# A router product turned round: weights stationary in four column groups, partial sums folded by stacked identities

## The reference

```python
x = x + gate1 * (concat(y_A, y_B) @ w_out)
h = rmsnorm(x, g_norm2) * (1.0 + scale2) + shift2
probs = softmax(h @ w_router)                 # 16 experts
gates, idx = top_k(swapaxes(probs, 1, 2), cap)  # each expert picks: 64 latent, 16 context tokens
# 16 SwiGLU experts on the picked rows, added back with their gates
```

## Time and profile before

| | |
|---|---|
| median of 3 runs | 897.25 us (895.78 to 897.99) |
| the profiled execution | 896.64 us |
| its span on the core | 894.2 us |
| TensorE busy | 97% of the span |
| granted TensorE clock, mean | 0.995 |
| output projection and routers of tiles 0 to 3 | from about 265 to 325 us |
| choice of the largest | 325.7 to 338.4 us |
| experts | from 344.8 us to the end |

### The profile page before, as it was taken

How to read it: one execution, slowest core, us unless ns; L and a number is a source line. 1 busy time by engine, 2 the same in 40 slices (tenths; PEclk the granted TensorE clock), 3 DMA queues, 4 the chain that set the end, 5 groups by cost and what they waited for, 6 DMA issues and landing times.

```text
span 894.2 us, 14324 instructions
## 1 busy us (share of the span) xinstructions
PE 869.4 (97%) x6263; PEld 484.3 (54%) x6263; DVE 288.2 (32%) x592; ACT 226.4 (25%) x437; POOL 84.5 (9%) x83
## 2 busy tenths in 40 slices
PE   5999999999999999999999999999999999999995
PEld 4798999999998885333333333333333333333332
DVE  3476553767465564201101101101101101101125
ACT  5557633462351224101101101101101101101123
POOL 1000000000000012011011011011011011011022
PEclk9999999999999999999999999999999999999998
DMA  9845714523248348999999999999999999999973
GB/s 350 298 151 185 256 65 151 200 96 119 82 145 357 132 153 321 362 386 409 399 384 411 409 386 410 399 386 412 394 381 413 395 384 412 395 381 410 422 253 132
DMA packets 48577, 272.37 MB, mean 305 GB/s; under 512 B 6283, under 2 KB 8367, under 8 KB 36229
## 3 DMA queue, kind: packets, MB, share of 16 engines
q1 hardware_dynamic: 40716, 255.15, 72.3%
q0 software_dynamic: 6128, 10.89, 5.2%
q10 hardware_dynamic: 1672, 5.43, 1.6%
HBM read 257.95 MB, written 14.55 MB: 305 GB/s over the span
## 4 chain that ended last, share of the span: by engine, by line
PE 93%; DVE 3%; ACT 1%; issue 1%; DMA 1%; ACTq 0%; POOLq 0%; POOL 0%; DVEq 0%
PE pair L2143 25%; PE pair L1799 16%; PE pair L2188 13%; PE pair L2173 13%; PE pair L2201 6%; PE pair L2014 5%; PE pair L1739 2%; PE pair L1834 2%; PE pair L2102 1%; PE pair L2158 1%; PE pair L1778 1%; PE pair L1942 1%; PE pair L2027 1%; PE pair L2164 1%; PE pair L1847 1%
## 5 line engine op out<-in xcount | busy, mean ns | idle before, releaser
L2143 PE MATMUL pair<-ring,xT 128*64 128x512 f32 x1024 | 223.9, 594 | 0.3 <-ACT xT L1017 0.3
L2143 PEld LDWEIGHTS pair<-ring,xT 128*64 128x64 f32 x1024 | 71.9, 137 | 142.1 <-issue 141.9
L2173 PE MATMUL pair<-ring,xT 128*32 128x512 f32 x1024 | 116.5, 595 | 0.9 <-DVE xT L1604 0.9
L2188 PE MATMUL pair<-ring,aT 128*64 128x512 f32 x512 | 116.9, 598 | 0.0
L1039 ACT ACTIVATE act_l<-pair 128x512 f32<-128x512 f32 x16 | 9.6, 597 | 290.8 <-PE pair L2143 290.8
L1613 DVE TENSOR_TENSOR act_l<-act_l,pair 128x512 f32<-128x512 f32 x16 | 11.0, 686 | 207.9 <-ACT act_l L1039 207.9
L1799 PE MATMUL pair<-hT_hi,w_hi 128*128 128x320 f32 x320 | 75.4, 317 | 1.5 <-DVE hT_lo L1183 1.5
L1799 PE MATMUL pair<-hT_lo,w_hi 128*128 128x320 f32 x320 | 73.1, 310 | 0.0
L1799 PE MATMUL pair<-hT_hi,w_lo 128*128 128x320 f32 x320 | 72.9, 309 | 0.0
L2188 PEld LDWEIGHTS pair<-ring,aT 128*64 128x64 f32 x512 | 34.0, 136 | 69.5 <-issue 68.2
L2173 PEld LDWEIGHTS pair<-ring,xT 128*32 128x32 f32 x1024 | 30.2, 109 | 73.1 <-issue 73.1
(11 more groups left out here) (299 smaller groups left out, 937.0 us busy)
## 6 DMA issues: line engine op xcount, KB each, us to landing
ring<-in_w_gate SPq DMA_DIRECT2D x32, 2048.0 KB, 29.2
ring<-in_w_up SPq DMA_DIRECT2D x32, 2048.0 KB, 18.1
ring<-in_w_down SPq DMA_DIRECT2D x32, 2048.0 KB, 23.7
p1w<-in_w_mod SPq DMA_DIRECT2D x12, 2048.0 KB, 10.6
p1w<-in_w_in SPq DMA_DIRECT2D x5, 2048.0 KB, 8.0
x_sb<-in_x_sample SPq DMA_DIRECT2D x8, 512.0 KB, 5.2
p1w<-in_w_out SPq DMA_DIRECT2D x2, 2048.0 KB, 8.3
hn<-xr ACTq DMA_DIRECT2D x5, 512.0 KB, 2.6
```

The lines of the kernel that those rows point to most:

```text
L2143: ins = mm(ps[64 * n:64 * n + 64, :], xt[:, kk, 0:CAP_L], w[:, j, n * 512:(n + 1) * 512], start=kk == 0, stop=kk == KC - 1)
L2173: ins = mm(ctx_ps[32 * g:32 * g + 32, :], xt[:, kk, CAP_L:96], w[:, j, n * 512:(n + 1) * 512], start=kk == 0, stop=kk == KC - 1)
L2188: ins = mm(y_ps[0][r:r + 64, :], aT[:, j, 64 * fh:64 * fh + 64], wd[:, j, n * 512:(n + 1) * 512], start=fh == 0 and j == 0, stop=fh == 1 a ...
```

## The change

The router is turned round. The scaled weights, padded with zeros from 16 to 32 columns, become stationary, and the 128 turned tokens move. Row k goes to column group k mod 4, so a tile's result comes as four partial sums in four bands of 32 PSUM rows, experts along partitions (job `lp{t}`). These 128x128 are copied to SBUF (`parts`: by ScalarE for tiles 0, 1, 2 and 4, by VectorE for tile 3), and one further product with `parts` stationary and `group_sum` moving (four stacked identities, 128x16) adds the four bands and turns the result back (job `lg{t}`, in the second bank of the same pair). `group_sum` is made by a reduction of the identity. `normalise(3)` and `store_rows(3)` move behind the first softmax. Around `router(4)` four more identity products are put in. The semaphore `silu_zero` is folded into `const_ready`. In the diff below the parts follow in the order: list of jobs, memory, ScalarE, VectorE, TensorE.

```diff
-    jobs += ["wo0", "wo1", "x2T0", "x2T1", "lg0", "wo2", "lg1", "x2T2", "wo3", "lg2", "x2T3", "lg3", "pT", "wo4", "g2_0", "g2_1", "ixT", "x2T4", "lg4", "pTc", "ixTc", "pcT"]
+    jobs += ["wo0", "wo1", "x2T0", "x2T1", "lp0", "wo2", "lg0", "lp1", "lg1", "x2T2", "wo3", "lp2", "lg2", "x2T3", "lp3", "lg3", "pT", "wo4", "g2_0", "g2_1",
+             "ixT", "x2T4", "lp4", "lg4", "pTc", "ixTc", "pcT"]
...
-        w_scaled = at("w_scaled", R_V + 4096, [P, KC, 2, E])
+        w_scaled = at("w_scaled", R_V + 4096, [P, KC, 2, 32])
+        group_sum = at("group_sum", R_V + 6144, [P, E])
+        parts = at("parts", R_V + 6656, [P, 2, P])
...
+            def router_parts(t):
+                act.wait_ge(job_done, job(f"lp{t}") + 1)
+                if t >= 2:
+                    act.wait_ge(job_done, job(f"lg{t - 2}") + 1)
+                a.activation(parts[:, t % 2, :], pairs[PAIR[f"lg{t}"]][:, 0:P], ACT.Copy).then_inc(part_ready, 1)
+
             for t in range(NT - 1):
                 second_norm(t)
                 if t + 2 < NT:
                     mixed_hi(t + 2)
+                if t:
+                    router_parts(t - 1)
                 if t == NT - 2:
                     h2_turn(t)
                     a.activation(smax[:, 0, NT - 1:NT], one_col[:, 0:1], ACT.Exp)
-                store_rows(t)
                 if t < NT - 2:
+                    store_rows(t)
                     h2_turn(t)
...
             a.activation(probs[:, 0:NT - 1, :], probs[:, 0:NT - 1, :], ACT.Exp).then_inc(exp_ready, 1)
+            store_rows(NT - 2)
...
             h2_turn(NT - 1, 1)
+            router_parts(NT - 1)
...
+            dve.wait_ge(const_ready, 2)
+            v.memset(w_scaled[:, :, :, E:], 0.0)
+            v.tensor_reduce(group_sum[:, :], ident[:, :].rearrange("p (g e) -> p e g", g=4)[:, 0:E, :], AX.X, ALU.add)
             for i in range(2):
-                ins = v.tensor_tensor(w_scaled[:, :, i, :], w_router_sb[:, :, :],
+                ins = v.tensor_tensor(w_scaled[:, :, i, 0:E], w_router_sb[:, :, :],
                                       scale2[:, :, i:i + 1].to_broadcast([P, KC, E]), ALU.mult)
...
-                v.scalar_tensor_tensor(out=logits[:, t, :], in0=pp[:, 0:E], scalar=rms[:, 5, t:t + 1],
+                v.scalar_tensor_tensor(out=logits[:, t, :], in0=pp[:, 512:512 + E], scalar=rms[:, 5, t:t + 1],
...
                 inverse_of(rms, slice(t, t + 1), EPS)
-                normalise(t)
                 if t < NT - 2:
+                    normalise(t)
                     high_chunks(t)
                 if t:
                     router_row(t - 1)
+            dve.wait_ge(job_done, job(f"lp{NT - 2}") + 1)
+            dve.wait_ge(job_done, job(f"lg{NT - 4}") + 1)
+            v.tensor_copy(parts[:, (NT - 2) % 2, :], pairs[PAIR[f"lg{NT - 2}"]][:, 0:P]).then_inc(part_ready, 1)
             router_row(NT - 2)
...
+                if turn == 1:
+                    normalise(NT - 2)
                 pp = result(dve, ("pT", "pTc")[turn - 1])
...
                 for k in range(KC):
-                    ins = mm(pp[:, 0:E], h2T[t % 2][:, k, :], w_scaled[:, k, vec(t), :], start=k == 0, stop=k == KC - 1)
-                end(ins, f"lg{t}")
+                    g = 32 * (k % 4)
+                    ins = mm(pp[g:g + 32, 0:P], w_scaled[:, k, vec(t), :], h2T[t % 2][:, k, :], start=k < 4, stop=k >= 4)
+                end(ins, f"lp{t}")
+
+            def router_sum(t):
+                pe.wait_ge(part_ready, t + 1)
+                pp = pairs[PAIR[f"lg{t}"]]
+                end(mm(pp[:, 512:512 + E], parts[:, t % 2, :], group_sum[:, :], start=True, stop=True), f"lg{t}")
...
             router(0)
             output_projection(2, 1)
+            router_sum(0)
             router(1)
-            output_projection(3, 0)
+            output_projection(3, 0, range(4))
+            router_sum(1)
+            output_projection(3, 0, range(4, KC))
             turn_tile(2)
             output_projection(3, 1)
             router(2)
             output_projection(4, 0, range(1))
+            router_sum(2)
             turn_tile(3)
             output_projection(4, 0, range(1, 2))
             router(3)
-            output_projection(4, 0, range(2, 5))
+            output_projection(4, 0, range(2, 3))
+            router_sum(3)
+            output_projection(4, 0, range(3, 5))
...
             keep_warm("lg4", 5)
             router(4)
+            for _ in range(4):
+                mm(pairs[PAIR["lg4"]][:, 512:512 + P], ident[:, :], ident[:, :], start=True, stop=True)
+            router_sum(4)
             keep_warm("pTc", 8)
```

More of the change, by code:

```diff
@@ L128, in claims_in_order @@
     names += [n for n in JOBS[JOBS.index("mod1"):JOBS.index("wo0")] if n not in OPENED and n not in LATE]
-    return names + LATE + JOBS[JOBS.index("wo4") + 1:]
+    return names + LATE + [n for n in JOBS[JOBS.index("wo4") + 1:] if n != "lp4"]
 CLAIMS = claims_in_order()
@@ L152 @@
 LAST_ON = place_jobs()
-assert sorted(CLAIMS) == sorted(JOBS)
+assert sorted(CLAIMS + [f"lp{t}" for t in range(NT)]) == sorted(JOBS)
 MOD_ORDER = [0, 2, 1, 3, 4, 9, 5, 10, 6, 11, 7, 8]
@@ L329, in build @@
         names = """job_done prm_in tail_in decay_in st_in const_ready mask_ready param_ready silu_ready o_root
-            silu_zero decay_zero modrow_ready mod_sum mod_ready scale_ready ss_ready root_ready
+            part_ready decay_zero modrow_ready mod_sum mod_ready scale_ready ss_ready root_ready
             xr_ready hT_low hT_high raw_even raw_odd hT_hi_ready hT_ready whi_ready wlo_ready yThi_ready yTlo_ready alow_ready qk_first qk_second abs_ready min_ready softplus_ready cum_ready
@@ L340, in build @@
         (job_done, prm_in, tail_in, decay_in, st_in, const_ready, mask_ready, param_ready, silu_ready, o_root,
-         silu_zero, decay_zero, modrow_ready, mod_sum, mod_ready, scale_ready, ss_ready, root_ready,
+         part_ready, decay_zero, modrow_ready, mod_sum, mod_ready, scale_ready, ss_ready, root_ready,
          xr_ready, hT_low, hT_high, raw_even, raw_odd, hT_hi_ready, hT_ready, whi_ready, wlo_ready, yThi_ready, yTlo_ready, alow_ready, qk_first, qk_second, abs_ready, min_ready, softplus_ready, cum_ready,
@@ L575, in link @@
                 pool.wait_ge(pool_chain, steps[0])
-            g.memset(silu_c[:, :, :], 0.0).then_inc(silu_zero, 1)
+            g.memset(silu_c[:, :, :], 0.0).then_inc(const_ready, 1)
             g.memset(eps_col[:, :], EPS)
@@ L708, in _ @@
             act.dma_start(param_rows[R_BA:R_BA + H, DK:P], b_a_b[0].rearrange("(h d) -> h d", d=DK)).then_inc(prm_in, 16)
-            act.wait_ge(const_ready, 1)
+            act.wait_ge(const_ready, 2)
             a.activation(smax[:, 0, 0:1], one_col[:, 0:1], ACT.Sqrt)
@@ L731, in _ @@
             act.wait_ge(param_ready, 1)
-            act.wait_ge(silu_zero, 1)
+            act.wait_ge(const_ready, 1)
             a.activation(silu_c[:, :, 0:2].rearrange("p k v -> p v k"),
@@ L1720, in turn_params @@
                 pe.wait_ge(prm_in, 160)
-                pe.wait_ge(const_ready, 1)
+                pe.wait_ge(const_ready, 2)
                 pp = claim(pe, "prm")
```

## The result

Sixteen runs of the changed kernel have a median of 899.9 us (897.0 to 901.6), sixteen of the kernel before 896.8 us (895.0 to 900.4). The ratio is 1.0029, with a 95% interval from 1.0018 to 1.0039: slower by 2.6 us (by the medians alone, 3.1), at the edge of the 0.3% within which I counted a time as the same. The forecast was 898.8 us, 1.5 us over the kernel before as it was measured then, the range 895.9 to 901.3. In what follows, a ratio and its interval compare a kernel with runs of the kernel before beside it.

A forecast was written before the change was run, and what follows sets the result against it. TensorE, 93% of the chain, was taken to bound the kernel; 3.6 us less TensorE work against about 5.1 us of new waits and lost cover gave +1.5 us on the 897.25 us median: 898.8 us, range 895.9 to 901.3.

The forecast's parts named there:

- The price of the router: New router on TensorE, 16 records: 0.6 us taken, lower bound 0.45, upper 1.02; old router 1.69 us.
- The sum: Product on TensorE adding the partial sums, with its change of shape: 0.25 us.
- the 3.6 us: TensorE work saved: 0.84 us each for tiles 0 to 2, 1.08 for tile 3; full saving a rival, 13%, 893.7 us.
- Tile 0 and tile 1: Logits row delays VectorE's wo2 reads; TensorE idle 1.6 us before wo3; tile 2's turning follows at 310.55, 0.5 us lost.
- Tile 2: TensorE idle 1.8 us at router_sum(2), behind ScalarE's square sum and root of tile 3; turning of tile 3 ends 321.5.
- Tile 3: router_row(3) starts at about 324.25 instead of 322.83 us, 1.4 us later, taken as 1.5 with hand-overs.
- seven hand-overs of 0.05 us: Hand-overs rounded away along the tiles' chain, some 0.05 us each at seven places; 1.4 us was taken as 1.5.
- The hidden parts: Memset, group_sum reduction and store of tile 3 covered; normalise(3) shows at most 0.1 us; router(4) still takes 1.9 us.
- the clock: Rival, 11%: new idle spells on TensorE lower the clock to 1.2 GHz; 901.3 us, with both spells 903.8.
- the signs that I had named: Wrong if sums of tiles 1, 2 start without wait, tile 3's turning ends before 320.0, or clock under 1.00, 300-345 us.
- the one idle spell of 1.55 us before 338.43: Argument against a falling clock: TensorE's idle spell during VectorE's rounds of choosing left the clock at 1.00.
- 2.5 us for one fall: Some 2.5 us of work in the chain doubled at 1.2 GHz, added to 898.8 us: 901.3 us.

The follow-up runs named there:

- changed, again: The changed kernel unaltered, run once more beside others on one chip: 899.1 us, ratio 1.0025.
- first wait filled: Changed kernel plus seven identity products in TensorE's new wait before the first product of wo3 only: 899.7 us, ratio 1.0021.
- both filled: Changed kernel plus seven identity products in each new TensorE wait, before wo3's first product and before tile 2's sum: 896.9 us, ratio 1.0002.
- both filled, again: The changed kernel with identity products in both new TensorE waits, run a second time: 897.4 us, ratio 1.0004.
- sum of tile 0 early: Changed kernel with tile 0's sum after the first row of wo2's second half instead of after the whole half: 896.9 us, ratio 1.0005.
- copies early: Changed kernel with ScalarE's copies of the parts of tiles 1 and 2 ahead of the square sums: 896.3 us, ratio 0.9996.
- both early: Changed kernel with tile 0's sum early, ScalarE's copies for tiles 1, 2 before next square sum, tile 1's sum after one row of wo3: 894.2 us, ratio 0.9972.
- both early, again: The version of the changed kernel with early sums and early copies, run a second time: 894.1 us, ratio 0.9972.
- and sum of tile 3: The version with early sums and early copies, plus tile 3's sum after two identity products instead of a row of wo4: 895.7 us, ratio 0.9974.
- moves alone: Kernel before, old router, with only normalise(3) and store_rows(3) moved behind the first softmax: 897.7 us, ratio 0.9997.

## Why the prediction was right, and where it fell short

The table has the stretch from `router(0)` to the turned probabilities in each profiled execution, and what followed until the end of the last product of the last expert.

| kernel | stretch, us | clock 300 to 325 | turned probabilities to first gathered rows | from there to the last expert's end | ratio to before |
|---|---|---|---|---|---|
| before | 29.62 | 1.00 | 20.01 | 539.05 | 1 |
| changed | 33.36 | falls twice | 19.96 | 540.08 | 1.0029 |
| changed, again | 31.00 | 1.00 | 19.94 | 539.06 | 1.0025 |
| first wait filled | 32.30 | falls once | 20.44 | 539.28 | 1.0021 |
| both filled | 31.00 | 1.00 | 19.94 | 539.05 | 1.0002 |
| both filled, again | 30.99 | 1.00 | 19.94 | 540.85 | 1.0004 |
| sum of tile 0 early | 29.63 | 1.00 | 19.94 | 539.05 | 1.0005 |
| copies early | 28.63 | 1.00 | 19.94 | 539.06 | 0.9996 |
| both early | 27.25 | 1.00 | 19.94 | 539.82 | 0.9972 |
| both early, again | 27.26 | 1.00 | 19.94 | 539.12 | 0.9972 |
| and sum of tile 3 | 27.15 | 1.00 | 20.67 | 539.70 | 0.9974 |
| moves alone | 29.62 | 1.00 | 20.01 | 541.59 | 0.9997 |

*The price of the router.* I took 0.6 us, between 0.45 and 1.02. The chain of the changed kernel has 0.57 us for 16 records, 0.036 us each. The sum, taken at 0.25, is 0.22 from its start to the next (300.63 to 300.85). TensorE's work did shrink by what was said. With copies and sums in better places, 2.4 of the 3.6 us arrive. The rest goes mainly to tile 3, whose copy and sum stand in the chain wherever they are put: from `router(3)` to the turned probabilities it is still 3.59 us (318.06 to 321.65), against 3.95 before.

*Tile 0 and tile 1.* Right: VectorE held 3.12 us at the logits row, TensorE 1.77 at `wo3` (I said 1.6) and, with the clock up, 0.24 at the sum of tile 1 (I had some 0.5). Moving one sum took 1.37 us of the stretch back, which shows it.

*Tile 2.* Right: 1.71 us at the sum, where I had 1.8. *Tile 3:* with the clock up, the stretch is 31.00 us, 1.38 longer; I added up 1.4 and took 1.5. The seven hand-overs of 0.05 us that I named would have made it nearly 1.8; adding only 0.1 for them was no sum, and nothing of them shows.

*The hidden parts.* Right. From the turned probabilities to the first gathered rows it is 19.94 to 20.01 us in all but two traces, in which the gather landed 6.0 and 6.2 us after its issue; the moves alone are worth nothing.

*The term that was mis-sized* is the clock, which I put at 1.00 in the sum and kept as a rival with 11%. By the signs that I had named, the profiled execution went against me in two: the clock fell below 1.00 between 300 and 345 us, and the sum of tile 1 started without a wait (307.68 us), since TensorE's own products before it ran at the lower clock and came later than the copy. The mechanism of the waits was right; the forecast left out what follows them in some executions, and the median lay inside the range because the range reached as far as one fall. The loss is 2.6 us where I gave 1.5.

I argued from the one idle spell of 1.55 us before 338.43, after which the clock held. That was one spell in one execution. It held after this spell in all twelve traces, but the new spells of 1.71 and 1.77 us, counted where they stand unfilled, were followed by the lower clock in three cases of seven: both in the changed kernel, one with the first wait filled, none in the changed kernel's second trace, with the sum of tile 0 early, or with the copies early. Whether the 0.2 us or what stands around a spell makes the difference was not tested.

Of the 28 runs of the changed kernel, 12 have a mean clock of 0.992 or less, and they are some 2.8 us slower than the others in both sets (901.0 against 898.2, 901.5 against 898.7). In the traces of the changed kernel and its filled versions the mean clock is 0.992 with two falls, 0.994 with one and 0.995 or 0.996 with none, so some of the other 16 may hold one fall; the mean can't tell, since the kernel before has 0.993 to 0.997. The price was mis-sized too: 2.5 us for one fall was too high, 1.06 and 1.30 is what the traces show, because less of the chain ran at the lower level each time than I had allowed, from about 303.5 to 307 and from 320.6 to 324 us, and a part of the first lay over TensorE's wait for ScalarE (0.24 us where the clock held). Two falls make 2.36 where I had said 5.0. With 9 of 16 and 3 of 12 runs in the slower group, 1.4 us of waits and 2.8 for the group would make 3.0 and 2.1 us; measured were 2.6 and 2.2 by the ratios, 3.1 and 1.5 by the medians. That is arithmetic and no proof. What shows the cause is that the filled waits bring the clock to 1.00 in two traces and the stretch to 31.00 us, and leave none of the 24 runs with both waits filled under 0.994.

*The Trainium skill.* The page "TensorE: Matmul & The Clock Gate" (section "Why this matters for your kernels") warns of idle gaps between bursts of products, but of longer ones than these. Here 1.77 and 1.71 us of idle were followed by a clock of 0.50 in the trace of the changed kernel, and the same gaps by 1.00 in the trace of its second series: shorter gaps can do it, and need not.

*What stays open.* With both waits filled the stretch is 1.4 us longer than before, but the two medians are only 0.0 and 0.7 us over the one before. So how the loss of 2.6 us divides between waits and clock is shown for the stretch, not for the median. The fastest of the 24 filled runs took 896.1 us, the fastest of 57 runs of the kernel before beside them 894.8, which fits the stretch but proves little: with the sum of tile 0 early, where the stretch is that of the kernel before, the fastest of 12 took 895.8. The last column but one of the table shows where much of the scatter is: the experts' part varies from 539.05 to 541.59 us between executions of kernels that do the same there. In the trace of the moves alone TensorE waits in it for a weight transfer (0.6 us) and for the gather of the context rows (0.4), in that of the second filled run for that gather (0.9). A third wait is near the end of the last expert, here in the profiled execution of the changed kernel:

```profile
886.83 0.35 PE L2155 MATMUL pair<-last,add_l 128*128 128x1 f32 x2 [0.98 <-ACT left_l L1079]
```

It is 1.23 us with the moves alone, 0.77 in the second filled run, and absent before. It comes where the four loads of the final rows (`x_sb<-sum_l`) landed late: their median from issue to landing is 7.0 to 9.0 us in the six traces without this wait, 9.1 in one with 0.22 us of it, and 9.6 to 10.4 in the five with 0.6 us or more. In the profiled execution of the changed kernel, then, 0.98 us of the time has nothing to do with its routers as far as the traces show. Whether a later start of the experts makes these waits rarer, and so gives part of the 1.4 us back, was not tried.

## What to carry to other kernels

Splitting a product into a faster product, a copy and a sum saved TensorE time here only when the copy stood early in the queue of the engine that makes it, and when nobody asked for the sum ahead of work that others need. Follow each new result through the lists of all engines, and place it by when its input is there, not by which tile it belongs to: here three places in lists were the difference between 2.6 us lost and 2.5 us gained (by the ratios). And when an added wait makes TensorE idle for a microsecond or two, count the clock after it as a cost that comes in some executions, or fill the wait with products that nobody reads.

## What was not expected of the hardware

- The same idle spell, 1.77 us, was followed by the lower clock in one execution and not in another, with the same kernel and the same order of work.
- With 32 stationary columns in four groups and 128 moving columns, float32 products come at 0.036 us a record, above the 0.028 us that a quarter of the 0.112 us for 512 columns would give. (The group of 256 columns in those rows has 61 records in 3.57 us because the window of the view ended in it. In a wider view of the same chain it has 64 in 3.59, so a record comes every 0.056 us and not every 0.059, as the prediction has it.)
- The change of shape costs little. After the new router with its 32 columns, the first product of the output projection is followed by the next after 0.34 us (294.97 to 295.31 in the version with early sums and early copies). After the old router, which has no column groups, it was 0.31 (296.87 to 297.18), and from product to product it is 0.23.
